# Hybrid encoder layer: the output weights are split into two halves piece by piece inside the attention loop

## What is computed

```python
def reference(x, norm_in, w_in, ..., w_out):
    xn = rms_norm(h, norm_in[l])
    proj = jnp.einsum('bsd,dn->bsn', xn, w_in[l])
    ...
    y_a = blocked_attention(q, k, v)            # 8 heads of 64, 2 kv heads
    ...
    y_b = blocked_attention(qb, kb, vb)         # 4 heads, 96 for q/k, 128 for v
    y = jnp.concatenate([y_a * jax.nn.silu(a_g), y_b * jax.nn.silu(b_g)], axis=-1)
    h = h + jnp.einsum('bsm,md->bsd', y, w_out[l])
```

## Time and profile before

| | |
|---|---|
| Median of 3 runs | 1583.99 us (1583.68 to 1584.9) |
| The profiled execution | 1581.66 us |
| Its span, first to last instruction | 1579.9 us |
| Mean granted TensorE clock | 0.997 of full speed |
| Busy in the span: PE, DVE, ACT, POOL | 1534.4, 1303.0, 1232.3, 586.0 us |
| DMA traffic | 162.51 MB, mean 103 GB/s |

### The profile page before, as it was taken

The page is one execution under the profiler, slowest core; times in us unless marked ns, Lnnn a source line. Parts: engine busy times, 40 slices in busy tenths (PEclk is TensorE's granted clock), DMA queues, the critical chain, the costliest instruction groups (busy, mean ns, idle before and its releaser), DMA issues.

```text
span 1579.9 us, 37686 instructions
## 1 busy us (share of the span) xinstructions
PE 1534.4 (97%) x13326; PEld 889.6 (56%) x13326; DVE 1303.0 (82%) x1947; ACT 1232.3 (78%) x1656; POOL 586.0 (37%) x506
## 2 busy tenths in 40 slices
PE   7999999999998999999999999999999999979999
PEld 3555555555553566566566556656655655644444
DVE  6886676776888988998898899899889889897764
ACT  8787667667657888888888888888888888877663
POOL 0100000000002665666666566666656656630000
PEclk9999999999999999999999999999999999999999
DMA  9344444453323543334323334323332422536663
GB/s 339 109 137 76 112 116 71 109 110 70 82 65 98 112 99 72 86 82 96 79 64 92 79 79 97 86 65 70 83 66 63 92 58 67 125 91 213 201 198 106
DMA packets 245540, 162.51 MB, mean 103 GB/s; under 512 B 65040, under 2 KB 226320, under 8 KB 245488
## 3 DMA queue, kind: packets, MB, share of 16 engines
q1 hardware_dynamic: 222128, 147.28, 37.2%
q10 hardware_dynamic: 22464, 13.63, 3.1%
q0 software_dynamic: 896, 0.93, 0.8%
HBM read 119.16 MB, written 40.93 MB: 101 GB/s over the span
## 4 chain that ended last, share of the span: by engine, by line
PE 56%; DVE 8%; issue 3%; ACT 0%; DVEq 0%; DMA 0%; POOLq 0%; SPq 0%
PE p_acc L2063 5%; PE p_st L2027 5%; PE p_st L2026 5%; PE p_acc L2067 4%; DVE hand_part L1864 4%; PE hand_mx L1994 4%; PE p_acc L2069 4%; PE p_acc L2068 3%; PE p_st L1507 3%; PE p_st L1508 3%; PE p_st L1510 3%; PE p_st L2029 3%; PE p_st L2030 3%; PE hand_mx L1996 3%; PE p_acc L2064 3%
## 5 line engine op out<-in xcount | busy, mean ns | idle before, releaser
L1776 POOL TENSOR_TENSOR p_pl<-p_p,p_ph 128x512 f16<-128x512 f32 x384 | 503.9, 1319 | 291.6 <-ACT p_ph L1815 232.3
L1864 DVE TENSOR_REDUCE hand_part<-hand_mx 128x2 f32<-128x1024 f32 x373 | 455.0, 1220 | 78.1 <-PE hand_mx L1994 60.0
L1806 ACT ACTIVATE p_p<-p_st 128x1024 f32<-128x1024 f32 x384 | 390.9, 1018 | 98.3 <-PE p_st L2034 50.2
L1194 PE MATMUL p_ring<-p_w_hi,p_xT 128*128 128x512 f16 (+3 forms) x1536 | 389.3, 339 | 7.5 <-DVE p_w_lo L902 5.0
L1815 ACT ACTIVATE p_ph<-p_p 128x1024 f16<-128x1024 f32 x336 | 355.2, 1057 | 18.4
L1892 DVE TENSOR_TENSOR p_pl<-p_p,p_ph 128x512 f16<-128x512 f32 x384 | 325.9, 849 | 5.4 <-ACT p_ph L1815 4.6
L1194 PE MATMUL p_ring<-p_w_lo,p_xT 128*128 128x512 f16 (+3 forms) x768 | 260.0, 339 | 0.0
L1194 PEld LDWEIGHTS p_ring<-p_w_hi,p_xT 128*128 128x128 f16 x1536 | 150.7, 98 | 127.1 <-DVE p_xT L860 5.6
L2063 PE MATMUL p_acc<-p_vas,p_ph 128*128 128x129 f16 x2048 | 207.9, 221 | 0.0
L2063 PEld LDWEIGHTS p_acc<-p_vas,p_ph 128*128 128x128 f16 x2048 | 180.6, 97 | 36.4 <-issue 14.1
L2064 PE MATMUL p_acc<-p_vas,p_pl 128*128 128x65 f16 x2048 | 201.1, 193 | 0.0
(11 more groups left out here) (196 smaller groups left out, 2364.8 us busy)
## 6 DMA issues: line engine op xcount, KB each, us to landing
p_vbs<-scratch_vb SPq DMA_DIRECT2D x16, 1028.0 KB, 6.3
p_xin<-in_x SPq DMA_DIRECT2D x16, 512.0 KB, 7.1
p_xcol<-in_x_cols SPq DMA_DIRECT2D x16, 512.0 KB, 6.7
scratch_g<-p_g SPq DMA_DIRECT2D x16, 512.0 KB, 3.4
p_kb<-scratch_kb SPq DMA_DIRECT2D x32, 256.0 KB, 5.4
p_vas<-in_x SPq DMA_DIRECT2D x16, 512.0 KB, 4.0
out<-p_ph SPq DMA_DIRECT2D x15, 512.0 KB, 2.8
out_gt<-scratch_g ACTq DMA_DIRECT2D x13, 512.0 KB, 3.4
```

Of the source, the lines that this page charges most:

```text
L1194: last = pe.matmul(ring_t[:, 0:w], a, b, start=(k == 0 and m == 0), stop=(k == len(steps) - 1 and m == len(terms) - 1))
L1776: pool.tensor_tensor(pl[:, s % NP, 1, :], p32[:, s % N32, QB:], ph[:, s % NP, 1, :], ALU.subtract).then_inc(s_lop, 1)
L1806: act.activation(p32[:, s % N32, :], st[:, s % 2, :, :].rearrange("p a b -> p (a b)"), ACT.Exp, scale=scale).then_inc(s_exp, 1)
L1864: dve.tensor_reduce(part[:, e // MPAIRS % 3, 2 * c:2 * c + 2], mx[:, :, :], AX, ALU.max).then_inc(s_red, 1)
```

## The change

The output weights are no longer split after the loop. Each turn i handles one piece of 128 rows by 512 columns: block `n % 8` of column half `n // 8`, n = i. SP loads it (256 KB) into a small `w_raw`. ACT makes its hi half at step 11, DVE its lo half at step 22 (at step 13 in the last turn), both into `w_new`, and SP copies `w_new` (256 KB, from one place of the on-chip memory to another) to its place in the full weights. In SP's list of a turn the copy and the load of the next piece stand between `store_y(i, 1)` and `max_rows(i + 1, 0)`, and the copy waits for DVE's lo half. The loads of 512 KB in the turns 1 to 8 are gone, and so is all splitting at the end of the last turn and after it.

In the last turn DVE makes the hi half in two more steps (14 and 21), gate and turn of output tile 0 stand one step earlier (16 and 17), and DVE moves eight of the 16 quadrants (steps 21, 22); ACT moves the other eight (steps 22, 23). ACT's moves of tile 1 stand ahead of its wait for the last store of y and of the first `silu`. In phase 1 `latent_lo(T15)` stands ahead of `rotate_heads(T14)`. A wait of SP for stores of the handover stands in turn 0 and not in turn 1.

```diff
@@ Output
-        self.w_raw = sb("w_raw", [P, KT, D])
+        self.w_raw = sb("w_raw", [P, QB])
+        self.w_new = sb("w_new", [P, 2, QB], F16)
...
+        self.w = [split(kept[:, 0:8 * D]), split(sb("w_right", [P, 8 * D], F16)[:, :])]
@@ phase 1, DVE
                 else:
+                    latent_lo(T15, 1)
                     rotate_heads(T14, 0)
-                    latent_lo(T15, 1)
@@ output stage, ACT
             if first and h == 1:
-
+                y_moves(t, h, True)
                 act.wait_ge(o.s_yst, SEQ // QB * HB * 48)
             if not (first and h == 0) and not (last and h == 1):
                 silu(t + 1, 1 - h, i if h == 0 else i + 1)
@@ output stage, DVE
             if first and h == 0:
-                split_lo(0)
                 return
             if first:
                 low(1, 1)
                 y_moves(1, 1, True)
-                for k in range(1, KT // 2):
-                    split_lo(k)
                 gate(2, 0, 1)
@@ output stage, PE
             pe.wait_ge(s_ytd, t + 1)
-            if not (first and h == 0):
-                pe.wait_ge(s_yta, t)
+            pe.wait_ge(s_yta, t + 1)
             for c in range(2):
+                if first and h == 0:
+                    pe.wait_ge(o.s_win, (c + 1) * KT * 16)
...
-                    if first and h == 0 and k % 2 == 0:
-                        pe.wait_ge(s_wlo, c * (KT // 2) + k // 2 + 1)
@@ phase 2
+    DVE_HI_LAST = (5, 11, 14, 18, 21)
+    W_HI_AT, W_LO_AT, W_LO_LAST = 11, 22, 13
+    Y_MOVES_AT = {22: slice(0, 3), 23: slice(3, 8)}
@@ phase 2, SP
+            def load_piece(n):
+
+                cols = slice(n // KT * 512, n // KT * 512 + 512)
+                sp.dma_start(o.w_raw[:, :], w_rows[:, n % KT, cols]).then_inc(o.s_wout, 16)
+
+            def place_piece(n):
+
+                sp.wait_ge(o.s_wlo, n + 1)
+                sp.dma_start(o.w[n // KT][:, :, n % KT, :], o.w_new[:, :, :]).then_inc(o.s_win, 16)
...
                     load_vb(0)
+                    load_piece(0)
...
-                if i == 1:
+                if i == 0:
                     sp.wait_ge(hand.s_zst, PAIRS * ZST)
                 store_y(i, 1)
-                if 0 < i <= KT:
-                    sp.dma_start(o.w_raw[:, i - 1, :], w_rows[:, i - 1, :]).then_inc(o.s_wout, 16)
+                place_piece(i)
                 if more:
+                    load_piece(i + 1)
                     max_rows(i + 1, 0)
                     sp.wait_ge(s_st, i * HALF + HALF)
                     load_q(i + 1, 2)
@@ phase 2, ACT
-                if s in DVE_HI:
+                if s in dve_steps(i):
                     return
...
+                    if s == W_HI_AT:
+                        piece_hi(i, first)
...
+                    if last and s in Y_MOVES_AT:
+                        y_moves(Y_MOVES_AT[s])
...
+            def piece_hi(i, first):
...
+                    act.wait_ge(o.s_wout, i * 16 + 16)
+                    act.wait_ge(o.s_win, i * 16)
+                act.activation(o.w_new[:, 0, :], o.w_raw[:, :], ACT.Copy, scale=WS).then_inc(o.s_whi, 1)
...
             loop(act, body)
-            act.wait_ge(o.s_whi, 1)
-            split_w(0, range(1, 4))
-            act.wait_ge(s_pv, free.pv_grouped)
-            split_w(1, range(0, 2))
             copy_acc(N - 1, 2, False)
             high(1)
-            split_w(1, range(2, 4))
@@ phase 2, DVE
+                    if s == (W_LO_LAST if last else W_LO_AT):
+                        piece_lo(i)
+                    if last and s == 16:
+                        gate(0)
                     if last and s == 17:
-                        gate(0)
-                    if last and s == 18:
                         turn(0)
                     if last and s == 20:
                         low(0)
-                        split_w(0)
-                    if last and s in (21, 22, 23):
-                        y_moves(((0, 1), (2,), (3,))[s - 21], s == 23)
+                    if last and s in (21, 22):
+                        y_moves((s - 21,), s == 22)
...
+            def piece_lo(i):
+
+                dve.wait_ge(o.s_whi, i + 1)
+                dve.scalar_tensor_tensor(out=o.w_new[:, 1, :], in0=o.w_raw[:, :], scalar=WS, in1=o.w_new[:, 0, :],
+                                         op0=ALU.mult, op1=ALU.subtract).then_inc(o.s_wlo, 1)
...
             lo(N - 1, HALF - 1, False)
-            split_w(1)
-            split_w(2)
-            split_w(3)
             gate(1)
             turn(1)
```

More of the change, by code:

```diff
@@ L91, in __init__ @@
         sem = lambda n: ctx.enter_context(nc.semaphore("out_" + n))
-        self.w_raw = sb("w_raw", [P, KT, D])
-        half = lambda n: kept[:, n:n + 4 * D].rearrange("p (k c) -> p k c", k=KT)
+        self.w_raw = sb("w_raw", [P, QB])
+        self.w_new = sb("w_new", [P, 2, QB], F16)
         rows = lambda n: kept[:, n:n + 2 * D].bitcast(F32)
-        self.w_hi = half(0)
-        self.w_lo = half(4 * D)
+        split = lambda w: w.rearrange("p (s k c) -> p s k c", s=2, k=KT)
+        self.w = [split(kept[:, 0:8 * D]), split(sb("w_right", [P, 8 * D], F16)[:, :])]
         self.ya = rows(8 * D).rearrange("p (s h d) -> p s h d", s=2, h=HA)
@@ L106, in __init__ @@
         self.yT = part(12 * D, 4 * D).rearrange("p (h s k t) -> p h s k t", h=2, s=2, k=KT)
-        self.s_wout = sem("w_out_loaded")
+        self.s_wout = sem("w_piece_loaded")
+        self.s_win = sem("w_piece_in_place")
         self.s_whi = sem("w_hi")
@@ L1332, in __init__ @@
         flat = lambda b, n: b[:, 4 * n:4 * n + 4, :, :].rearrange("p n b q -> p (n b q)")
-        weights = lambda b: flat(b, 0).rearrange("p (k c) -> p k c", k=KT)
-        self.w_hi, self.w_lo = weights(ph), weights(pl)
         self.res = flat(ph, 1).bitcast(F32).rearrange("p (h c) -> p h c", h=2)
@@ L1346, in output_stage @@
     xr, res = free.xr, free.res
-    w_hi, w_lo = [o.w_hi, free.w_hi], [o.w_lo, free.w_lo]
-    w_raw = o.w_raw
+    w = o.w
     ya, yb, gt, yg = o.ya, o.yb, o.gt, o.yg
@@ L1351, in output_stage @@
     po = free.po
-    s_wlo, s_y, s_g, s_sg, s_yg = o.s_wlo, o.s_y, o.s_g, o.s_sg, o.s_yg
+    s_y, s_g, s_sg, s_yg = o.s_y, o.s_g, o.s_sg, o.s_yg
     s_yh, s_yl, s_ytr, s_ytd, s_yta = o.s_yh, o.s_yl, o.s_ytr, o.s_ytd, o.s_yta
@@ L1402, in silu, with y_moves @@
             act.activation(gt[:, h, :], gt[:, h, :], ACT.Silu).then_inc(s_sg, 1)
+        def y_moves(t, h, first):
+            act.wait_ge(s_yl, t + 1)
+            if not first:
+                act.wait_ge(s_po, t * 2 - 2)
+            for dst, src in o.moves(h, (2, 3)):
+                end = act.activation(dst, src, ACT.Copy)
+            end.then_inc(s_yta, 1)
         def tile(t, h, i, first, last):
@@ L1413, in tile @@
                 silu(t + 1, 1 - h, i if h == 0 else i + 1)
-            if not (first and h == 0):
[L1415 to L1420, removed]
+            if not first:
+                y_moves(t, h, False)
             if not last and not (first and h == 0):
@@ L1504, in tile @@
                 for k in range(KT):
-                    if first and h == 0 and k % 2 == 0:
-                        pe.wait_ge(s_wlo, c * (KT // 2) + k // 2 + 1)
-                    pe.matmul(po[h][c][:, :], yT[:, h, 0, k, :], w_hi[c][:, k, :], start=k == 0, stop=False)
-                    pe.matmul(po[h][c][:, :], yT[:, h, 0, k, :], w_lo[c][:, k, :], start=False, stop=False)
+                    pe.matmul(po[h][c][:, :], yT[:, h, 0, k, :], w[c][:, 0, k, :], start=k == 0, stop=False)
+                    pe.matmul(po[h][c][:, :], yT[:, h, 0, k, :], w[c][:, 1, k, :], start=False, stop=False)
                 for k in range(KT):
-                    mm = pe.matmul(po[h][c][:, :], yT[:, h, 1, k, :], w_hi[c][:, k, :], start=False, stop=k == KT - 1)
+                    mm = pe.matmul(po[h][c][:, :], yT[:, h, 1, k, :], w[c][:, 0, k, :], start=False, stop=k == KT - 1)
                 mm.then_inc(s_po, 1)
@@ L1590, in lo_done, with dve_steps @@
             eng.wait_ge(s_lo if b == 0 else s_lop, i * HALF + s + 1)
+        def dve_steps(i):
+            return DVE_HI_LAST if isinstance(i, int) and i == N - 1 else DVE_HI
         def hi_done(eng, i, s):
@@ L1595, in hi_done @@
                 i, s = i - 1, s + HALF
-            dve_before = len([c for c in DVE_HI if c < s])
-            if s in DVE_HI:
+            turn_hi = dve_steps(i)
+            dve_before = len([c for c in turn_hi if c < s])
+            if s in turn_hi:
                 eng.wait_ge(s_hid, i * len(DVE_HI) + dve_before + 1)
@@ L1841, in _, with y_moves @@
             act.activation(hand.zT[0:DB, 5:NCH, P:2 * P], turned[0][0:DB, :, :], ACT.Copy).then_inc(hand.s_outa, 1)
[L1842 to L1846, removed]
+            def piece_hi(i, first):
+                if first:
+                    act.wait_ge(o.s_wout, 16)
+                else:
+                    act.wait_ge(o.s_wout, i * 16 + 16)
+                    act.wait_ge(o.s_win, i * 16)
```

(12 more changed lines are left out.)

8 lines of the change are left out of this document (removed).

## The result

The changed kernel takes 1657.94 us (median of 4 runs, 1655.7 to 1659.24) against 1583.85 us: a ratio of 1.0465, 95% interval 1.0447 to 1.0483. It is slower by 74 us. The forecast was 1660.0, range 1634 to 1682. The profiled execution has a span of 1657.4 us at a mean granted clock of 0.982.

What follows compares the result with a forecast made beforehand. PE was taken to set the pace in phase 2. 1581.66 us + 87 for turn ends - 10.6 for the transition - 0.9 for phase 1 = 1657.2; with 2.3 to the median 1659.5, said as 1660, range 1634 to 1682.

Steps and rivals of the forecast that it cites:

- The main step: At each turn's end, row copies queue behind SP's wait for DVE's lo half; PE stalls, 5.8 us with clock loss, 15 times.
- Part 2: Rest of a turn: ACT's hi half moves an exponential by about 0.4 us but costs nothing; dropped loads give nothing back.
- The stall: At each turn's end PE stands still for 4.1 us because the second row lands at 1343.1, wanted at 1339.04.
- the prediction's signs: What the profile would show at turn ends, among it row copies landing above 3 us after issue.
- they stand behind 512 KB in their queue: At the turn's end, bytes ahead delay the row copies: 2.7 us over a tiny transfer, 1.35 us for each 256 KB.
- The clock term: Behind each of 15 turn-end stalls the clock falls to half, costing 1.7 us each.
- The transition: Going into the output stage, PE's waits of 3.29 and 4.59 us and clock falls go: 10.6 us credited of 11.3.
- `lo(21)` no longer arrives late: At the transition, DVE loses splits and half its moves, gets two hi halves, so PE's 3.29 us wait goes.
- Phase 1: PE's 2.34 us wait for `latent_lo(T15)` goes, but PE comes forward by only about 0.9 us; bounds 0 and 2.3.
- (d): Rival: row copies at turn ends still land in time, only the transition's gain is left: 1572.5 us; chance 0.04.
- (a): Rival: row copies don't queue behind the pieces, 2.7 + 1.7 us a turn: 1638.5 us; chance 0.14.
- (b): Rival: the turn-end stalls of 4.1 us come but the clock stays up: 1634 us; chance 0.05.

Runs made afterwards that it cites:

- e1: Changed kernel with the row copies of the next turn's maxima ahead of the copy into place and the load in SP's list: 1582.03 us.
- e2: As e1, but SP waits for DVE's lo half ahead of the row copies, with copy into place and load behind them: 1605.02 us.
- e3: Changed kernel with the row copies between the copy into place and the load of the next piece: 1630.01 us.
- e9: As e4, but each piece's load brings its columns twice, 512 KB in one transfer and not 256: 1676.9 us.
- e4: Changed kernel with the first piece's load issued ahead of the turns, not behind turn 0's key, query and value loads: 1651.83 us.
- e8: Changed kernel with row copies first, first piece loaded early, phase 1 order undone, and last-turn hi halves of steps 14 and 21 on ACT: 1573.15 us.
- e10: As e4, but DVE makes a piece's lo half at step 17 and not 22, SP's order unchanged: 1589.21 us.

## Why the prediction was right

**The main step held in kind and nearly in size.** "`max_rows(i + 1, 0)` is queued behind it": 15 waits of PE for the row copies, one per turn's end, and e1 takes them away by order alone. `piece_lo` took 0.69 us (0.7 said), fitted into DVE's gap, and the copy went out when it ended. A turn is 61.1 us long on average (near 62 said), and the mean clock is 0.982 (near 0.98 said). Part 2 held too: PE waited for ACT four times in all, 6.2 of 8.5 us in turn 0, so ACT's hi half costs nothing in the later turns.

**The stall was over-sized**: 4.1 us said, 3.42 measured. The working took the landing from the pair behind one load of 512 KB, 5.1 us after the first issue. It was 4.5 (1118.1 - 1113.65): the rows were issued 1.38 us behind the copy and not 1.1, but landed 2.7 and 2.5 us after issue, where the prediction's signs asked for more than 3. The taken-apart sum is 1.51 for the wait (e2), 0.77 for the copy, nearly all its issue (e3), and 1.14 for the load (after - e3), of which 0.7 is its issue (1114.33 to 1115.03) and 0.4 to 0.5 the later landing. The term that was mis-sized is "they stand behind 512 KB in their queue", priced at 1.35 us for each 256 KB. The copy's 256 KB cost next to nothing (e3) and the load's 256 KB 0.4 to 0.5; only a further 256 KB in the load cost the 1.3 (e9). Why the first 256 KB cost so much less than the next was not looked into, and no run has the load alone ahead of the rows. An issue costs 0.68 us here and not the 0.55 I spaced them by. The Trainium skill's page "DMA: Bandwidth & Descriptors", section "Bandwidth", had given an estimated 2.9 us of stall by its rate of 341 GB/s; the measured 3.42 lies between it and the rows' 4.1.

**The clock term was nearly right**: 15 falls of 1.7 us said, 25.5 in all; 14 came, 1.7 us each, 23.9 in all, the last of them in the last turn.

**Turn 0 was missed.** The text checked SP's list only for what the last pieces delay. It did not follow the added `load_piece(0)`: a new load at the end of a full queue, and an ACT wait at step 11 with all exponentials behind it. 6.1 us (e4). The rule for a moved or added transfer, who waits for it and what is queued behind the waiter, was applied to the copy and not to the first load.

**The transition was credited 10.6 and gave about 7.8**: 6.1 us from the last turn's first scores to the end, plus 1.7 for the clock fall that the last row wait brought into that stretch. The output stage gained 6.1 of it, as the 4.6 and 1.7 us had it. The step that failed is "`lo(21)` no longer arrives late": DVE still made PE wait 3.2 us in three pieces. Its two added hi halves are part of that: without them the kernel gains 2.3 us (e8), and this wait falls by 1.0.

**Phase 1 was credited 0.9 and gives nothing.** The wait of 2.34 us goes, as said, but PE then waits 2.65 us for DVE at the turn of the last keys, where it had no wait before. "DVE's chain doesn't get shorter" was right, but it gets longer: DVE stands still for 1.15 us ahead of its lo latents where it used to rotate heads. It waits there for ACT's hi latents, whose second part (L672) ends at 460.66 in the changed kernel:

```profile
460.17 0.49 ACT L672 ACTIVATE p_lat_hi<-p_ckv,p_lstat 128x256 f16<-128x256 f32 x1
```

```profile
460.76 0.62 DVE L921 SCALAR_TENSOR_TENSOR p_lat_lo<-p_cq,p_lstat,p_lat_hi 128x384 f16<-128x384 f32 x1 [1.15 <-issue]
```

These errors partly cancel: stall and clock 87 said, 75.2 measured (51.3 and 23.9); turn 0 +6.1; transition 10.6 said, 7.8 measured; phase 1 0.9 said, none measured. The mechanism was foreseen; that the forecast of 1660 came within 2.1 us of the median is in part luck, since a stall that was too large covered the wait in turn 0 and two gains that did not come. Of the rivals, (d) was wrong by a wide margin, (a) held for the copy's half of the bytes and for most of the load's, (b) holds for a wait of 1.5 us and not for 3.4.

## What to carry to other kernels

A small transfer with a deadline should stand ahead of anything in its queue that waits for a later step of another engine: here the order of three lines is worth 76 us of 1658, with the same work for every engine (e1). When work moves into a loop, subtract, per queue, the time at which the waiting item is released from the time at which the next consumer needs what stands behind it, and do it for the first and the last turn apart from the middle. A gap in which an engine waits for PE anyway is free room: the 0.69 us of the lo half cost nothing at step 22 (e1), and 12 us of PE's waits over the loop at step 17, where DVE has no gap (e10).

## What the hardware showed that was not expected

PE's idle time and the clock behind it, counted over the 15 turn ends: it fell behind none of the waits of 1.5 us (e2), 7 of those of 2.3 us (e3), 14 of those of 3.4 us (the changed kernel) and all of those of 4.7 us (e9). A fall lasted 3.4 us at half clock and cost 1.7; one in e3 and ten in e9 lasted 6.8. After the wait of 2.65 us in phase 1 it fell in six traces and not in three, after the one of 2.3 us in two of four. So two kernels with the same waits, and likely two executions of one kernel, can differ by one fall. The runs of e1 spread over 4.4 us (1579.84 to 1584.27), with a mean clock of 0.995 or 0.996 in the three slowest and 0.998 in the fastest.

A copy of 256 KB within on-chip memory landed 2.6 us after issue and did not delay a 1 KB transfer issued 0.7 us behind it in the same queue (2.0 us to landing as ever), while with a load of 256 KB between them it landed after 2.7 and 2.5 us, and with one of 512 KB after 3.9 and 4.1.
